# Query projection of a two-block model: keys' split, compressed branch's transposes and scores in other places of the order

## The chip, the cores and the metric

One core of a Trainium2 chip runs the whole program. The metric is the time on the device in microseconds, the median of the runs of one kernel.

## What is computed

Two transformer blocks over 512 tokens of width 1024. The change lies in the attention of the first block's second layer, which has 16 query heads in 4 groups and three branches: a compressed one over 31 blocks of keys, a selected one and a window. With 512 tokens, 8 selected blocks of 64 are all blocks, and the window of 512 takes in all that is past. Cut to what matters:

```python
u = h @ w_q
q = (u[..., :N_HEADS * D_QK] * (D_QK ** -0.5)).reshape(B, S, G, HPG, D_QK)
gates = jax.nn.sigmoid(u[..., N_HEADS * D_QK:] + gate_bias).reshape(B, S, G, HPG, N_BRANCH)
q_rope = apply_partial_rope(q)
...
s_c = jnp.einsum('tghd,cgd->tghc', qn_t, kc_b).astype(jnp.float32)
p_c = masked_softmax(s_c, mask_c)
o_c = jnp.einsum('tghc,cgv->tghv', p_c.astype(vc_b.dtype), vc_b)
...
return g_t[..., 0:1] * o_c + g_t[..., 1:2] * o_s + g_t[..., 2:3] * o_w
```

## The kernel before

The program is one long list of instructions for each engine, written out by hand, with semaphores between them. A product in single precision is made of three: both operands are split into a high part (rounded, on ScalarE) and a low part (the rest, on VectorE), and TensorE adds high x high, low x high and high x low (`three`, lines 619 to 621). The weights come in panels of 1 MB through SyncE's queue into two buffers `a_raw`; `high_a` rounds a panel (line 1451), `low_a` makes its low part (line 2034), and TensorE waits for that (`a_ready`).

**The query projection** has eight panels (pairs of heads, p = 0 to 7, `A_Q + p`). For each, TensorE makes two halves of 24 products, j = 0 and 1, each into a bank of PSUM. VectorE's `evict_q(p)` takes each half out in two instructions, `qb` (line 2439) and `tmp` for the rotation (line 2442). ScalarE copies `qb` (line 1727). GpSimd's `rotate_q(p)` turns the first 24 dimensions of both halves in four instructions (lines 3040 and 3044); ScalarE's `high_q(p)` rounds the pair (`q_hi`, line 1702), VectorE's `low_q(p)` makes the low part (`qb_lo`, line 2448), and GpSimd's `store_q(p)` writes both to memory, from where `stage_q` fetches a pair for the attention. `high_q(p)` and `low_q(p)` stand one pair later in their queues, before the eviction of pair p + 1. The keys `kx` of the two other branches have been made earlier and are split into `kx_hi` (ScalarE, line 1733) and `kx_lo` (VectorE, line 2484), in two pieces.

**The compressed branch** runs between the halves, a group (two pairs) at a time, over one bank, `bank[7]`. For group g: `scores_c(g)` on TensorE (line 963), `copy_scores_c` on ScalarE (`ct`, line 1706), `turn_c` on TensorE, four transposes (line 970), `peak_c` on VectorE (four instructions, lines 2457 to 2461, into `pc`), `expo_c` on ScalarE (line 1710), `weigh_c` on VectorE (five instructions, lines 2465 to 2470), `back_c` on TensorE, four transposes (line 976), `turned_c` on ScalarE (`ptc`, line 1714). Group g's scores come behind the first half of pair 2g + 2 and group 3's in the attention.

**The attention** has 48 units n (a head in three parts); TensorE does `scores(n + 2)`, `turn(n)` (line 1029) and every second unit `outputs` (line 1054), VectorE `peak` (lines 2499 to 2504) and `scale` (line 2515), ScalarE `expo` (line 1741) and `turned` (line 1752). At its start TensorE does

```python
scores(0)
scores_c(GROUPS - 1)
scores(1)
keep(6, 6)
```

where `keep(b, n)` is n filler products into bank b (line 615).

## Time and profile before

| | us |
|---|---|
| median of 3 runs | 2221.01 |
| the runs | 2217.12, 2221.01, 2221.11 |
| the profiled execution | 2217.61 |
| its span in the profile | 2215.8 |

The profile is of one execution, and all its times count from the start of its span. The span lacks 1.8 us of what the device reports for the same execution. PE stands for TensorE, PEld for its weight loads, DVE for VectorE, ACT for ScalarE, POOL for GpSimd. A row of a timeline has the start, the duration, the engine and line, what was written and read, and in brackets how long the engine had been idle and what ended that.

### The profile page before, as it was taken

What the parts mean: (1) busy time and instruction counts of PE and PEld (TensorE: products, weight loads), DVE (VectorE), ACT (ScalarE), POOL (GpSimd) and SP (SyncE); (2) the same over time, 40 slices, a digit from 0 to 9 for tenths busy, and PEclk for the clock granted to TensorE, in tenths of its full rate; (3) what the DMA queues carried; (4) which work ended last, traced back from release to release, by engine and by line L of the source; (5) the groups of instructions that cost most, each with busy time, mean ns of one, the idle gap of its engine ahead of it and who ended that gap; (6) DMA issues with size and microseconds to landing.
All of it is one profiled execution on the core that took longest, in us unless ns stands there. A gap on an engine that the chain in (4) does not pass through costs nothing.

```text
span 2215.8 us, 27265 instructions
## 1 busy us (share of the span) xinstructions
PE 2148.4 (97%) x10514; PEld 1607.1 (73%) x10514; DVE 1270.7 (57%) x1697; ACT 838.2 (38%) x1258; POOL 274.1 (12%) x227
## 2 busy tenths in 40 slices
PE   7999999999999999999999999999999999899998
PEld 6787788888878877777788888877778885233346
DVE  6776855555587678775655555587674463000028
ACT  4556622222253445664422222364442332121243
POOL 1334300000010154000100000010000012222220
PEclk9999999999999999999999999999999999999999
DMA  5222323222224342112322222121122144999961
GB/s 192 88 102 96 114 77 113 85 94 105 78 70 161 124 148 66 39 35 86 126 97 102 85 105 94 66 76 58 58 96 114 58 167 195 414 410 401 376 239 57
DMA packets 60750, 291.84 MB, mean 132 GB/s; under 512 B 13872, under 2 KB 14256, under 8 KB 32582
## 3 DMA queue, kind: packets, MB, share of 16 engines
q1 hardware_dynamic: 41312, 258.49, 30.6%
q0 software_dynamic: 18096, 29.31, 4.4%
q10 hardware_dynamic: 1248, 2.76, 0.3%
q8 instruction: 63, 1.03, 0.2%
q14 instruction: 31, 0.25, 0.0%
HBM read 322.18 MB, written 20.38 MB: 155 GB/s over the span
## 4 chain that ended last, share of the span: by engine, by line
PE 76%; DVE 11%; DMA 5%; ACT 3%; issue 3%; POOL 1%; SPq 0%; ACTq 0%; POOLq 0%; DVEq 0%
PE psum L619 20%; PE psum L621 20%; PE psum L620 20%; PE psum L1353 4%; PE psum L1377 3%; DMA panel<-w_m 3%; PE psum L1054 2%; DVE a_lo L2034 1%; DMA over_panel<-w_m,over_row 1%; PE psum L1029 1%; PE psum L1320 1%; ACT a_hi L1451 1%; PE psum L767 1%; DVE xc L2175 1%; DMA expert_out<-h 1%
## 5 line engine op out<-in xcount | busy, mean ns | idle before, releaser
L619 PE MATMUL psum<-hn_hi,a_hi 128*128 128x512 f32 (+1 forms) x1592 | 631.5, 397 | 7.8 <-DVE hn_lo L2074 3.2
L621 PE MATMUL psum<-hn_hi,a_lo 128*128 128x512 f32 (+1 forms) x1592 | 622.5, 391 | 0.0
L620 PE MATMUL psum<-hn_lo,a_hi 128*128 128x512 f32 (+1 forms) x1592 | 620.2, 390 | 0.0
L619 PEld LDWEIGHTS psum<-hn_hi,a_hi 128*128 128x128 f32 (+1 forms) x1592 | 297.6, 187 | 79.7 <-issue 9.2
L621 PEld LDWEIGHTS psum<-hn_hi,a_lo 128*128 128x128 f32 (+1 forms) x1592 | 297.4, 187 | 68.9
L620 PEld LDWEIGHTS psum<-hn_lo,a_hi 128*128 128x128 f32 (+1 forms) x1592 | 297.4, 187 | 67.7 <-issue 2.4
L2034 DVE TENSOR_TENSOR a_lo<-a_raw,a_hi 128x2048 fp32r<-128x2048 f32 (+1 forms) x110 | 251.7, 2288 | 79.6 <-ACT a_hi L1451 79.0
L1451 ACT ACTIVATE a_hi<-a_raw 128x2048 fp32r<-128x2048 f32 (+1 forms) x110 | 205.2, 1867 | 82.6 <-PE psum L621 70.2
L2118 DVE TENSOR_TENSOR h<-h,psum 128x512 f32<-128x512 f32 x176 | 120.1, 686 | 79.8 <-PE psum L621 79.7
L3006 POOL TENSOR_TENSOR sq<-sq 128x512 f32<-128x512 f32 x6 | 9.0, 1506 | 1151.4 <-ACT sq L1464 1151.4
L2933 DVE TENSOR_TENSOR xhid<-xsg,psum 128x256 f32<-128x256 f32 x24 | 10.1, 421 | 239.9 <-ACT xsg L1984 239.9
L619 PE MATMUL psum<-hid_hi,b_hi 128*128 128x512 f32 x352 | 139.0, 395 | 2.0 <-DVE h L2118 1.9
L621 PE MATMUL psum<-hid_hi,b_lo 128*128 128x512 f32 x352 | 138.0, 392 | 0.0
L1613 ACT ACTIVATE sg<-sg 128x512 f32<-128x512 f32 x44 | 27.8, 632 | 288.3 <-DVE sg L2287 288.3
L620 PE MATMUL psum<-hid_lo,b_hi 128*128 128x512 f32 x352 | 136.7, 388 | 0.0
L1353 PE MATMUL psum<-panel,xw 128*64 128x512 f32 x512 | 115.1, 603 | 2.4 <-ACT xw L1954 2.4
L2292 DVE TENSOR_TENSOR hid<-sg,psum 128x512 f32<-128x512 f32 x44 | 30.2, 687 | 117.2 <-PE psum L621 117.1
L1615 ACT ACTIVATE hid_hi<-hid 128x512 fp32r<-128x512 f32 x44 | 27.8, 632 | 180.9 <-DVE hid L2292 180.9
L1458 ACT ACTIVATE b_hi<-b_raw 128x1024 fp32r<-128x1024 f32 x64 | 66.9, 1050 | 59.6 <-PE psum L621 57.4
L1353 PEld LDWEIGHTS psum<-panel,xw 128*64 128x64 f32 x512 | 36.2, 138 | 70.1 <-issue 70.1
L2040 DVE TENSOR_TENSOR b_lo<-b_raw,b_hi 128x1024 fp32r<-128x1024 f32 x64 | 80.0, 1257 | 7.3 <-ACT b_hi L1458 7.2
L619 PEld LDWEIGHTS psum<-hid_hi,b_hi 128*128 128x128 f32 x352 | 66.2, 188 | 16.7 <-issue 2.5
(524 smaller groups left out, 3337.1 us busy)
## 6 DMA issues: line engine op xcount, KB each, us to landing
a_raw<-w_a SPq DMA_DIRECT2D x116, 1024.0 KB, 4.9
panel<-w_m SPq DMA_DIRECT2D x96, 1024.0 KB, 14.0
b_raw<-w_b SPq DMA_DIRECT2D x64, 512.0 KB, 3.3
q_scratch<-q_hi POOLq DMA_DIRECT2D x7, 384.0 KB, 3.4
q_scratch<-qb_lo POOLq DMA_DIRECT2D x7, 384.0 KB, 4.6
q_hi<-q_scratch POOLq DMA_DIRECT2D x7, 384.0 KB, 4.0
q_lo<-q_scratch POOLq DMA_DIRECT2D x7, 384.0 KB, 4.7
out_t<-h SPq DMA_DIRECT2D x7, 256.0 KB, 2.0
```

Source lines behind the costliest of these rows:

```text
L619: pe.matmul(out, w_hi, x_hi, start=first, stop=False)
L620: pe.matmul(out, w_hi, x_lo, start=False, stop=False)
L621: return pe.matmul(out, w_lo, x_hi, start=False, stop=last)
L1054: mm = pe.matmul(bank[6 + at % 2][side * DV:(side + 1) * DV, t * P:(t + 1) * P], w, x, start=i == 0, stop=i == len(steps) - 1)
L1353: mm = pe.matmul(bank[v][rows, :], xw[:, v, k, rows], w[half][:, k % 4 * 2 * EFF:(k % 4 + 1) * 2 * EFF], start=k == 0, stop=k == KT - 1)
L1377: mm = pe.matmul(bank[4 + 2 * v + hb][rows, :], xturn[:, v, f * P + half * SLOTS:f * P + (half + 1) * SLOTS], w[half][:, f * D + hb * 512: ...
L1451: act.activation(a_hi[s % 2][:, 0:w], a_raw[s % 2][:, 0:w], ACT.Copy).then_inc(a_rounded, 1)
L1458: act.activation(b_hi[s % 2][:, :], b_raw[s % 2][:, :], ACT.Copy).then_inc(b_rounded, 1)
L2034: V.tensor_tensor(a_lo[s % 2][:, 0:w], a_raw[s % 2][:, 0:w], a_hi[s % 2][:, 0:w], ALU.subtract) \
L2040: V.tensor_tensor(b_lo[s % 2][:, :], b_raw[s % 2][:, :], b_hi[s % 2][:, :], ALU.subtract) \
L2118: V.tensor_tensor(h[:, m, :], h[:, m, :], bank[4 + m % 4][:, :], ALU.add).then_inc(y_free, 1)
L2292: V.tensor_tensor(hid[:, f, :], sg[:, f, :], ps[1][:, :], ALU.mult).then_inc(tile_free, 2)
```

## The change

- The keys' split moves from pairs 3 and 4 to pairs 0 and 1, on ScalarE and VectorE.
- `turn_c(g)` moves from behind the second half of pair 2g + 2 to behind the first half of pair 2g + 3; `peak_c(g)` from pair 2g + 2 to pair 2g + 3, `expo_c`, `weigh_c` and `back_c` to pair 2g + 4 (`back_c` behind its second half), `turned_c` to pair 2g + 5.
- `back_c` writes to bank 6 for groups 0 to 2, bank 7 for group 3. `scores_c(g)` then waits for `peak_c(g - 1)` where it waited for `turned_c(g - 1)`.
- `weigh_c(2)`, `back_c(2)` and `turned_c(2)` stand in the attention, `expo_c(2)` before `expo(0)`; the filler products come after `back_c(2)` and go to bank 5.
- In the attention `expo_c(3)` stands at unit 1 (was 2), `weigh_c(3)` at 2 (was 3), `back_c(3)` and `turned_c(3)` at 3 (were 5).

```diff
--- before.py
+++ after.py
@@ -495,6 +495,15 @@
                 return pt_ready, 10 * at + i + 5
             return late_pt_ready, 2 * at + i - 3
 
+        C_ACT = [("copied", 0), ("exp", 0), ("copied", 1), ("turned", 0), ("exp", 1), ("copied", 2), ("turned", 1),
+                 ("exp", 2), ("copied", 3), ("turned", 2), ("exp", 3), ("turned", 3)]
+
+        BACK_C = [6, 6, 6, 7]
+
+        def c_acts(what, g):
+
+            return C_ACT.index((what, g)) + 1
+
         def half_of(half):
             return slice(half * SLOTS, (half + 1) * SLOTS)
 
@@ -957,7 +966,7 @@
                 if g == 0:
                     pe.wait_ge(cmp_done, 2)
                 else:
-                    pe.wait_ge(c_act, 3 * g)
+                    pe.wait_ge(c_dve, 2 * g - 1)
                 for c in range(HPG):
                     pe.wait_ge(base_ready, 8 + 4 * g + c + 1)
                     mm = pe.matmul(bank[7][c * CBLOCK:(c + 1) * CBLOCK, :], kct[:, g * NCMP:g * NCMP + CBLOCK],
@@ -965,15 +974,17 @@
                 mm.then_inc(csc_ready, 1)
 
             def turn_c(g):
-                pe.wait_ge(c_act, 3 * g + 1)
+                pe.wait_ge(c_act, c_acts("copied", g))
                 for t in range(NT):
                     mm = pe.transpose(bank[7][:, t * P:(t + 1) * P], ct[:, t * P:(t + 1) * P], ident)
                 mm.then_inc(ctr_ready, 1)
 
             def back_c(g):
                 pe.wait_ge(c_dve, 2 * g + 2)
+                if 0 < g < GROUPS - 1:
+                    pe.wait_ge(c_act, c_acts("turned", g - 1))
                 for t in range(NT):
-                    mm = pe.transpose(bank[7][:, t * P:(t + 1) * P], pc[:, t, :, :].rearrange("p h c -> p (h c)"), ident)
+                    mm = pe.transpose(bank[BACK_C[g]][:, t * P:(t + 1) * P], pc[:, t, :, :].rearrange("p h c -> p (h c)"), ident)
                 mm.then_inc(ctr_ready, 1)
 
             for p in range(1, NPAIR):
@@ -981,10 +992,12 @@
                 pe.wait_ge(a_ready, s + 1)
                 for j in range(2):
                     product(tile_bank(s, j, s)[:, :], s, j * P, 2 * P, P, hh, hl).then_inc(tile_ready, 1)
-                    if p % 2 == 0:
-                        (turn_c if j else scores_c)(p // 2 - 1)
-                    elif j and p >= 3:
-                        back_c((p - 3) // 2)
+                    if j == 0 and p % 2 == 0:
+                        scores_c(p // 2 - 1)
+                    if j == 0 and p % 2 and p >= 3:
+                        turn_c((p - 3) // 2)
+                    if j == 1 and p % 2 == 0 and p >= 4:
+                        back_c(p // 2 - 2)
 
             def scores(n):
                 u, hd, slot = unit(n)
@@ -1035,9 +1048,8 @@
                 pair = PAIR_AT[at]
                 g = pair // 2
                 if u == 0:
-                    pe.wait_ge(c_act, 3 * (g + 1))
-                    if at == 1:
-                        pe.wait_ge(c_act, 3 * GROUPS)
+                    if at < 2:
+                        pe.wait_ge(c_act, c_acts("turned", GROUPS - 2 + at))
                     if at >= 2:
                         pe.wait_ge(o_split, at - 1)
                 for side in range(2):
@@ -1066,15 +1078,16 @@
             scores(0)
             scores_c(GROUPS - 1)
             scores(1)
-            keep(6, 6)
+            back_c(GROUPS - 2)
+            keep(5, 6)
             for n in range(NUNIT):
                 if n + 2 < NUNIT:
                     scores(n + 2)
                 if n == 0:
                     turn_c(GROUPS - 1)
-                if n == 5:
+                turn(n)
+                if n == 3:
                     back_c(GROUPS - 1)
-                turn(n)
                 if n % 2 == 0 and n >= 2:
                     outputs(n // 2 - 1)
             pe.wait_ge(a_ready, A_WO + 1)
@@ -1711,26 +1724,26 @@
 
             def turned_c(g):
                 act.wait_ge(ctr_ready, 2 * g + 2)
-                act.activation(ptc[:, g, :], bank[7][:, :], ACT.Copy).then_inc(c_act, 1)
+                act.activation(ptc[:, g, :], bank[BACK_C[g]][:, :], ACT.Copy).then_inc(c_act, 1)
 
             for p in range(NPAIR):
                 if p:
                     high_a(A_Q + p + 1)
-                if p % 2 and p >= 3:
-                    expo_c((p - 3) // 2)
                 if p % 2 == 0 and p >= 4:
-                    turned_c(p // 2 - 2)
+                    expo_c(p // 2 - 2)
                 if p:
                     high_q(p - 1)
+                if p % 2 and p >= 5:
+                    turned_c((p - 5) // 2)
                 for j in range(2):
                     act.wait_ge(base_ready, 8 + 2 * p + j + 1)
                     act.activation(qb[:, 2 * (p % 2) + j, 1, :], qb[:, 2 * (p % 2) + j, 0, :], ACT.Copy) \
                        .then_inc(base_copied, 1)
-                    if j == 0 and p % 2 == 0 and p:
-                        copy_scores_c(p // 2 - 1)
-                if p in (3, 4):
+                if p % 2 == 0 and p:
+                    copy_scores_c(p // 2 - 1)
+                if p < 2:
                     act.wait_ge(rope_done, 8)
-                    act.activation(kx_hi[:, p - 3, :, :], kx[:, p - 3, :, :], ACT.Copy).then_inc(k_rounded, 1)
+                    act.activation(kx_hi[:, p, :, :], kx[:, p, :, :], ACT.Copy).then_inc(k_rounded, 1)
 
             def expo(n):
                 act.wait_ge(mx_done, n + 1)
@@ -1755,19 +1768,20 @@
                 act.wait_ge(o_ready, 3 * at + 3)
                 act.activation(hn_hi[:, PAIR_AT[at], :], bank[6 + at % 2][:, :], ACT.Copy).then_inc(o_rounded, 1)
 
-            turned_c(GROUPS - 2)
+            expo_c(GROUPS - 2)
             expo(0)
             copy_scores_c(GROUPS - 1)
             expo(1)
+            turned_c(GROUPS - 2)
             for n in range(NUNIT):
                 turned(n)
                 if n + 2 < NUNIT:
                     expo(n + 2)
                 if n == 0:
                     high_q(NPAIR - 1)
-                if n == 2:
+                if n == 1:
                     expo_c(GROUPS - 1)
-                if n == 5:
+                if n == 3:
                     turned_c(GROUPS - 1)
                 if n % 6 == 1 and n > 6:
                     high_out(n // 6 - 1)
@@ -2472,17 +2486,13 @@
             for p in range(NPAIR):
                 if p:
                     low_a(A_Q + p + 1)
-                if p % 2 and p >= 3:
-                    weigh_c((p - 3) // 2)
+                if p % 2 == 0 and p >= 4:
+                    weigh_c(p // 2 - 2)
                 if p:
                     low_q(p - 1)
                 evict_q(p)
-                if p % 2 == 0 and p >= 2:
-                    peak_c(p // 2 - 1)
-                if p in (3, 4):
-                    V.wait_ge(k_rounded, p - 2)
-                    V.tensor_tensor(kx_lo[:, p - 3, :, :], kx[:, p - 3, :, :], kx_hi[:, p - 3, :, :], ALU.subtract) \
-                     .then_inc(k_split, 1)
+                if p % 2 and p >= 3:
+                    peak_c((p - 3) // 2)
                 if p == 0:
                     V.wait_ge(cmp_w2, 2)
                     V.wait_ge(rows_zero, 1)
@@ -2491,6 +2501,9 @@
                                             .rearrange("p (g c) -> p g c", g=GROUPS))
                     ins.then_inc(cmp_done, 1)
                     V.wait_ge(small_out, 3)
+                if p < 2:
+                    V.wait_ge(k_rounded, p + 1)
+                    V.tensor_tensor(kx_lo[:, p, :, :], kx[:, p, :, :], kx_hi[:, p, :, :], ALU.subtract).then_inc(k_split, 1)
 
             def peak(n):
                 v, u, x = n % 2, unit(n)[0], ast[:, n % 4, :]
@@ -2528,6 +2541,7 @@
                  .then_inc(o_split, 1)
 
             peak(0)
+            weigh_c(GROUPS - 2)
             peak(1)
             scale(0)
             for n in range(NUNIT):
@@ -2541,7 +2555,7 @@
                     peak_c(GROUPS - 1)
                 if n == 1:
                     low_q(NPAIR - 1)
-                if n == 3:
+                if n == 2:
                     weigh_c(GROUPS - 1)
                 if n % 6 == 1 and n > 6:
                     low_out(n // 6 - 1)
```

Three places of the order, first VectorE in pairs 0 and 1 (`kx_lo` is the keys' low part, `a_lo` the low part of a panel, `qb_lo` that of a pair of queries). Before:

```order
L2490 COPY vcz<-psum 31x4x64 x3
L2034 TENSOR_TENSOR a_lo<-a_raw,a_hi 128x2048 [waits a_rounded,small_out]
L2448 TENSOR_TENSOR qb_lo<-qb,q_hi 96x2x512 [waits queries_rounded]
L2439 SCALAR_TENSOR_TENSOR qb<-psum,rn 96x512 [waits tile_ready]
L2442 SCALAR_TENSOR_TENSOR tmp<-psum,cs 24x512 [waits rope_done]
L2439 SCALAR_TENSOR_TENSOR qb<-psum,rn 96x512 [waits tile_ready]
L2442 SCALAR_TENSOR_TENSOR tmp<-psum,cs 24x512 [waits rope_done]
```

And with the change:

```order
L2500 COPY vcz<-psum 31x4x64 x3
L2506 TENSOR_TENSOR kx_lo<-kx,kx_hi 96x2048 [waits keys_rounded,small_out]
L2048 TENSOR_TENSOR a_lo<-a_raw,a_hi 128x2048 [waits a_rounded]
L2462 TENSOR_TENSOR qb_lo<-qb,q_hi 96x2x512 [waits queries_rounded]
L2453 SCALAR_TENSOR_TENSOR qb<-psum,rn 96x512 [waits tile_ready]
L2456 SCALAR_TENSOR_TENSOR tmp<-psum,cs 24x512 [waits rope_done]
L2453 SCALAR_TENSOR_TENSOR qb<-psum,rn 96x512 [waits tile_ready]
L2456 SCALAR_TENSOR_TENSOR tmp<-psum,cs 24x512 [waits rope_done]
L2506 TENSOR_TENSOR kx_lo<-kx,kx_hi 96x2048 [waits keys_rounded]
L2048 TENSOR_TENSOR a_lo<-a_raw,a_hi 128x2048 [waits a_rounded]
```

The two `kx_lo` now stand directly before the `a_lo` of panels 2 and 3; the rest of the piece is as it was.

VectorE from pair 7 into the attention (`pc` and `cst` belong to the compressed branch, `ast` to the attention's units). Before:

```order
L2465 TENSOR_REDUCE cst<-pc 128x16 [waits c_act]
L2466 TENSOR_SCALAR cst<-cst 128x16 [waits dve_step]
L2467 RECIPROCAL cst<-cst 128x16 [waits dve_step]
L2469 TENSOR_TENSOR cst<-cst,gates 128x16 [waits dve_step]
L2470 TENSOR_TENSOR pc<-pc,cst 128x512 [waits dve_step]
L2448 TENSOR_TENSOR qb_lo<-qb,q_hi 96x2x512 [waits queries_rounded]
L2439 SCALAR_TENSOR_TENSOR qb<-psum,rn 96x512 [waits tile_ready,csc_ready,q_stored1]
L2442 SCALAR_TENSOR_TENSOR tmp<-psum,cs 24x512 [waits rope_done]
L2439 SCALAR_TENSOR_TENSOR qb<-psum,rn 96x512 [waits tile_ready]
L2442 SCALAR_TENSOR_TENSOR tmp<-psum,cs 24x512 [waits rope_done]
L2499 TENSOR_REDUCE ast<-psum 128x2 [waits sc_ready]
```

And with the change:

```order
L2456 SCALAR_TENSOR_TENSOR tmp<-psum,cs 24x512 [waits rope_done]
L2471 TENSOR_TENSOR pc<-psum,cn 128x512 [waits ctr_ready]
L2473 TENSOR_REDUCE cst<-pc 128x16 [waits dve_step]
L2474 TENSOR_SCALAR cst<-cst 128x16 [waits dve_step]
L2475 TENSOR_TENSOR pc<-pc,cst 128x512 [waits dve_step]
L2512 TENSOR_REDUCE ast<-psum 128x2 [waits sc_ready]
L2514 TENSOR_REDUCE ast<-psum 128x2
L2479 TENSOR_REDUCE cst<-pc 128x16 [waits c_act]
L2480 TENSOR_SCALAR cst<-cst 128x16 [waits dve_step]
L2481 RECIPROCAL cst<-cst 128x16 [waits dve_step]
L2483 TENSOR_TENSOR cst<-cst,gates 128x16 [waits dve_step]
L2484 TENSOR_TENSOR pc<-pc,cst 128x512 [waits dve_step]
```

`peak_c(2)` (the first four rows behind `tmp`) now stands between the last eviction and the attention's first unit, and `weigh_c(2)` (the last five) behind that unit's `peak`.

TensorE at the start of the attention, with the change (`qb,kct` are the compressed scores of group 3, `kx` and `q` the attention's, `cn,pc` the transposes of `back_c(2)`):

```order
L972 MATMUL psum<-qb,kct 32x512 [waits base_ready,c_dve]
L972 MATMUL psum<-qb,kct 32x512 [waits base_ready] x3
L628 MATMUL psum<-kx_hi,q_hi 128x256 [waits tile_free]
L629 MATMUL psum<-kx_lo,q_hi 128x256
L630 MATMUL psum<-kx_hi,q_lo 128x256
L628 MATMUL psum<-kx_hi,q_hi 128x512
L629 MATMUL psum<-kx_lo,q_hi 128x512
L630 MATMUL psum<-kx_hi,q_lo 128x512
L1031 MATMUL psum<-masks 128x256
L1031 MATMUL psum<-masks 128x2x128
L987 MATMUL psum<-cn,pc 128x128 [waits c_act,c_dve]
L987 MATMUL psum<-cn,pc 128x128 x3
```

Before, the first of these rows waited for `c_act` (`turned_c(2)`) and not for `c_dve` (`peak_c(2)`), and the `cn,pc` rows stood ahead of the attention's first scores.

## Rows read from the trace of the kernel before

**Rows 1.** Page, head and part 1: busy us, share of the span, instructions
```profile
span 2215.8 us, 27265 instructions
...
PE 2148.4 (97%) x10514; PEld 1607.1 (73%) x10514; DVE 1270.7 (57%) x1697; ACT 838.2 (38%) x1258; POOL 274.1 (12%) x227
```

**Rows 2.** Waits of TensorE, 755 to 900 us: total, times, longest (us)
```profile
PE psum L970 <- ACT ct L1706: 3.0, 2, 2.5
```

**Rows 3.** Timeline of TensorE, 784 to 864 us: start, us, line, operation, idle before
```profile
785.49 0.50 PE L619 MATMUL psum<-hn_hi,a_hi 128*128 128x512 f32 x1
...
791.11 0.60 PE L970 MATMUL psum<-cn,ct 128*128 128x128 f32 x4
...
791.46 0.48 PE L619 MATMUL psum<-hn_hi,a_hi 128*128 128x512 f32 x1
...
817.88 0.66 PE L970 MATMUL psum<-cn,ct 128*128 128x128 f32 x4 [2.52 <-ACT ct L1706]
...
858.49 1.07 PE L963 MATMUL psum<-qb,kct 96*32 96x512 f32 x8 [0.83 <-ACT ptc L1714]
...
860.88 2.76 PE L615 MATMUL psum<-cn 128*128 128x256 f32 x12
...
863.28 0.53 PE L619 MATMUL psum<-kx_hi,q_hi 96*128 96x384 f32 x1
```

**Rows 4.** Windows: length, busy us of the five rows of engines, PEclk, DMA share, GB/s
```profile
49.20:54.40 5.20, 5.18 (x18) 3.80 (x19) 1.10 (x1) 2.51 (x4) 2.94 (x2) 0.50 0.55 195
...
819.00:822.40 3.40, 3.40 (x10) 2.58 (x10) 3.30 (x5) 3.39 (x2) 3.16 (x3) 0.53 0.45 118
...
872.00:876.00 4.00, 4.00 (x46) 3.25 (x45) 2.63 (x6) 2.75 (x7) 0.00 (x0) 1.00 0.02 4
...
876.07:896.92 20.85, 19.76 (x190) 16.20 (x189) 16.70 (x39) 14.11 (x44) 1.31 (x2) 1.00 0.18 39
```

**Rows 5.** Timeline of GpSimd, 766 to 815 us
```profile
770.43 3.17 POOL L3044 TENSOR_TENSOR qb<-tmp,sq 24x512 f32<-24x512 f32 x1 [0.17 <-POOL sq L3040]
...
802.60 0.63 POOL L3053 DMA_DIRECT2D q_hi<-q_scratch  x1
...
806.62 5.55 POOL L3040 TENSOR_TENSOR sq<-qb,cs 24x512 f32<-24x512 f32 x1
```

**Rows 6.** Instructions on tile tmp, 760 to 870 us: min/median/max in ns
```profile
L3044 POOL TENSOR_TENSOR qb<-tmp,sq x16: 1253/1286/3171, 767.7 to 861.0; 24x512 f32<-24x512 f32 x16
```

**Rows 7.** Timeline of VectorE, 766 to 860 us
```profile
774.73 1.22 DVE L2448 TENSOR_TENSOR qb_lo<-qb,q_hi 96x1024 fp32r<-96x1024 f32 x1 [2.28 <-ACT q_hi L1702]
...
805.94 2.86 DVE L2484 TENSOR_TENSOR kx_lo<-kx,kx_hi 96x2048 fp32r<-96x2048 f32 x1 [1.78 <-ACT kx_hi L1733]
...
808.72 2.28 DVE L2034 TENSOR_TENSOR a_lo<-a_raw,a_hi 128x2048 fp32r<-128x2048 f32 x1
...
829.82 1.22 DVE L2448 TENSOR_TENSOR qb_lo<-qb,q_hi 96x1024 fp32r<-96x1024 f32 x1
...
841.13 1.22 DVE L2448 TENSOR_TENSOR qb_lo<-qb,q_hi 96x1024 fp32r<-96x1024 f32 x1 [2.27 <-ACT q_hi L1702]
...
848.08 0.69 DVE L2461 TENSOR_TENSOR pc<-pc,cst 128x512 f32<-128x512 f32 x1
...
851.99 0.68 DVE L2465 TENSOR_REDUCE cst<-pc 128x16 f32<-128x512 f32 x1
...
854.03 1.21 DVE L2448 TENSOR_TENSOR qb_lo<-qb,q_hi 96x1024 fp32r<-96x1024 f32 x1
...
858.04 0.42 DVE L2499 TENSOR_REDUCE ast<-psum 128x2 f32<-128x256 f32 x1
```

**Rows 8.** Timeline of ScalarE, 766 to 860 us
```profile
813.65 1.06 ACT L1702 ACTIVATE q_hi<-qb 96x1024 fp32r<-96x1024 f32 x1 [5.47 <-POOL qb L3044]
```

**Rows 9.** Timeline of TensorE, its stops elsewhere: idle time in brackets
```profile
49.22 0.76 PE L774 MATMUL psum<-xc_hi,a_hi 64*128 64x512 f32 x1 [3.75 <-issue]
...
871.34 0.87 PE L1029 MATMUL psum<-cn,pm_b 128*128 128x128 f32 x6 [1.69 <-DVE pm_b L2515]
```

## The prediction

> **What bounds the kernel now.** I read four views, in this order. The page's first part says whose time the span is: TensorE is busy 97% of 2215.8 us [rows 1], so only what TensorE waits for can be won. The waits of TensorE from 755 us to 900 us, the stretch of the query projection and the start of the attention, say what there is, above all 3.0 us in two waits of the transposes (L970) for `ct` [rows 2]. The timeline of TensorE shows where and when: the long one, 2.52 us, stands before the transposes of group 1 at 817.88, and the 0.83 us before the last compressed scores at 858.49 [rows 3]. The windows with the granted clock show a second loss behind the long wait: 0.53 in 819.0 to 822.4, that is half of 2.4 GHz [rows 4]. Three hi/lo products there are 0.6 us longer each, about 1.6 us in all. So at most 2.52 + 0.48 + 1.6 + 0.83 = 5.4 us can go, of 2217.61.
>
> Then I ask what was late. `ct` of group 1 stands in ScalarE's queue behind a copy that needs pair 4's eviction, that behind `low_q(3)` on VectorE, that behind `q_hi` at 813.65, which had waited 5.47 us for GpSimd [rows 8]. GpSimd's rotation of pair 3 had one instruction of 5.55 us at 806.62 [rows 5], where its like have a median of 1.29 [rows 6]: it ends 1.2 us behind VectorE's `kx_lo` and `a_lo`, which ran back to back from 805.94 to 811.0 [rows 7]. So there is a ring: `low_q(p-1)`, eviction of pair p, store and rotation on GpSimd, `q_hi` on ScalarE, `low_q(p)`. Its length is the distance of two `qb_lo` rows, 11.3 us (829.82 to 841.13) with one ordinary `a_lo` in GpSimd's way, and 12.9 us (841.13 to 854.03) where `peak_c`, `a_lo` and `weigh_c` lie in VectorE's queue between them [rows 7]. A pair on TensorE takes two halves of 5.6 us (785.49 to 791.11) plus 0.35 us per group of transposes and 1.0 per compressed scores (1.07 in the row at 858.49) [rows 3], 11.4 to 12.6 us. The ring is as long as TensorE's pair, and it is this ring that I follow through the change.
>
> **The change, part by part.** No instruction is added or removed on TensorE, VectorE or GpSimd, nor on ScalarE; what changes is where they stand and what they wait for.
>
> *Keys' split in pairs 0 and 1.* `kx_hi` (1.9 us) delays `a_hi` by as much, and TensorE needs those panels 3 us later still, so that costs nothing; if that cover went, it would be 1.9 us a panel. On VectorE `kx_lo` (2.3 us alone) now lies directly before `a_lo`. GpSimd's blocked instruction at 770.43 took 3.17 us behind one `a_lo` [rows 5]; with `kx_lo` ahead of it it ends 2.2 us later. `low_q(0)`, at 774.73 [rows 7], goes to 776.9. In pair 1 the instruction is blocked by both, as at 806.62: 4.24 us instead of 1.87, and the interval to `low_q(1)` is 11.3 + 2.4 = 13.7 us.
>
> Here the Trainium skill speaks otherwise. In "SBUF — State Buffer", section "Who interferes with whom", a VectorE instruction with two SBUF inputs and a GpSimd instruction that reads SBUF exclude each other, whoever is first holding the ports "for the whole instruction". By that GpSimd would be let in after `kx_lo`; the row at 806.62 shows it held over both. The sum goes by the row, the page's rule is rival 2.
>
> *The ring after that.* To `low_q(2)` 11.3; to `low_q(3)` with `peak_c(0)`, `a_lo`, `weigh_c(0)` between them, as in the 12.9 row, and `stage_q(0)` on GpSimd: between 12.9 and 12.9 + 1.3 (two DMA issues of 0.63) [rows 5], and I take 13.0, since VectorE sets that interval and not GpSimd; then 11.3, 12.9, 11.3. Sum from 776.9: 13.7 + 11.3 + 13.0 + 11.3 + 12.9 + 11.3 = 73.5, so `low_q(6)` begins at 850.4, 3.6 us earlier than the 854.03 of before. The kernel loses its two late `kx_lo` and wins 3.6 us on VectorE.
>
> *TensorE in the projection.* It starts pair 3 at 791.1 without the transposes before it and would need 11.44 us for each odd pair and 12.6 for each even one: 3 x 11.44 + 2 x 12.6 = 59.5, to 850.6. The transposes wait for copies half a panel old: `ct` of group 1 is written at about 819.5, they come at 822, so the 2.52, the 0.48 and the 1.6 us of the clock go. But `scores_c(g)` now waits for `peak_c(g-1)`, which ends 7.64 us behind the start of the `low_q` before it (841.13 to 848.77) [rows 7]. For group 1 that is 801.9 + 7.6 = 809.5 where TensorE arrives at 808.0: 1.5 us of new wait. For group 2 826.2 + 7.6 = 833.8 against 833.6: 0.2. The other bank for `back_c` is free for them all and costs nothing.
>
> *The passage into the attention, which decides.* `peak_c(2)` now stands on VectorE behind the eviction of the last pair: 850.4 + 7.6 = 858.0. TensorE has done the projection at 852.3 and `scores(0)` at 853.6, and then stands before `scores_c(3)` until 858.0: 4.4 us. Behind it in the queue are `scores(1)`, `back_c(2)` and the six filler products. VectorE goes on with `peak(0)` (1.05 us, its first row at 858.04) and `weigh_c(2)` (2.1, from 851.99 to 854.03) [rows 7], to 861.2; `back_c(2)` waits for it, 0.4; the fillers take 2.4 (860.88 to 863.28) [rows 3]; `scores(2)` begins at 864.0. Before it was 863.28. **+0.7 us**: the bank's wait of before (858.49) and the new one (858.0) are at the same place, and `weigh_c(2)`, formerly under the projection, now stands before the fillers.
>
> *The clock.* The nearest row to a stop of 4.4 us is that of 3.75 us before 49.22 [rows 9]: the clock is at 0.50 for 5.2 us under work behind it [rows 4]; behind 2.52 us it was 3.4 us, and behind the 1.69 us before 871.34 [rows 9] it stayed at 1.00 [rows 4]. Bounds: 0 and 3.4 us (6.8 us at half). I take the 3.75 row: in 5.2 us TensorE does 2.6 us of work, so at 863.2 it is where it would be at 861.4 without the fall (0.8 us of it is wait anyway). **+1.8 us.**
>
> *The last group in the attention.* `weigh_c(3)` one unit earlier, `back_c(3)` two. TensorE is idle for 1.09 us of the 20.85 us from 876.07 [rows 4], so 1 us is the bound on either side; VectorE's 2.1 us before `peak(5)` may add 0.7 at `turn(4)`, and what left later units gives it back: 0.
>
> Sum: 0.7 + 1.8 = +2.5, 2217.61 + 2.5 = 2220.1 us in the terms of the profiled execution. Its time lies 3.4 us under the median of the runs shown, 2221.01, so the prediction for a median is 2223.5 us. Two of the four times lie at 2217 and two at 2221, a scatter larger than the effect; 0.2%, 4.4 us, is what a measurement of this kernel can tell from no change.
>
> **The rivals.**
> 1. *No fall of the clock.* The stop begins at another moment than that before 49.22 did. For it: 1.7 us in the attention brought none. Against: both stops over 2.5 us did. 2221.01 + 0.7 = 2221.7.
> 2. *GpSimd is let in between `kx_lo` and `a_lo`.* Both early delays shrink by 2.3, but `a_lo` then stands behind GpSimd's 1.3: 1.0 us each, `peak_c(2)` ends at 856.0, `scores(2)` at 862.0, -1.3, with the clock's 1.8: 2221.5. This is the rule of the SBUF page above; row 806.62 is against it.
> 3. *TensorE regains the lead.* If the ring is shorter than my intervals, the floor is the last half of the projection: 850.9, then eviction 1.4 and `peak_c` 2.9, 855.2; `scores(2)` at 861.2, -2.1, with a stop short enough for no fall: 2218.9. The order of VectorE's queue excludes more; to pass -4.4 something that I put at nothing has to give as well.
> 4. *Slower.* One mechanism: GpSimd's rotations of pairs 6 and 7 meet VectorE in `peak_c(2)` and `weigh_c(2)`, which now lie in their time. It decides if `stage_q` costs its full 1.2 and one rotation (1.3) holds a step of VectorE; the stop becomes 6.9 us, the clock's fall then lies wholly under work and costs 3.4 - 0.8 = 2.6. 0.7 + 1.2 + 1.3 + 2.6 = 5.8: 2226.8. For it: the two engines do exclude each other in the rows; against: `peak_c` of 3.5 us has such a hold in it already.
>
> **How the numbers follow.** Forecast 0.47, rival 1 0.17, rival 2 0.12, rival 3 0.12, rival 4 0.12. Likeliest: 2223.5. The range leaves out the slow end of rival 4 and the fast end of rival 3: 2217.5 to 2227.5. Slower by over 0.2% (above 2225.4) is rival 4 and a little of the forecast, 0.16; faster by over 0.2% (below 2216.6) is a part of rival 3, 0.07; the rest, 0.77, is within.
>
> **What would show it.** Right: no wait of `cn,ct` transposes on TensorE and no half clock at 819; a wait of about 1.5 us before `scores_c(1)`, one of about 4.4 us before `scores_c(3)` ended by VectorE's `pc`, one of 0.7 before `back_c(2)`, then half clock; two GpSimd instructions of 3 to 5 us in pairs 0 and 1; `scores(2)` within 3 us of 863.3. Wrong: `peak_c(2)` done before 855, or `scores(2)` before 861; a loss outside 755 to 900 us would be none of mine.

## The result and the profile after

The change has a median of 2225.38 us (2222.41 to 2231.92, 14 runs) beside 2222.23 us for the kernel before (2217.12 to 2226.42, 14 runs): a ratio of 1.0022, 95% interval 1.0013 to 1.0031, or 3 to 7 us slower. Two repetitions gave 1.0023 [1.0013, 1.0033] and 1.0006 [0.9994, 1.0018]. All 38 executions of the change together have a mean of 2225.80, all 123 of the kernel before 2221.97: a difference of 3.8 us, 0.17%. The profiled execution of the change took 2224.76 us. "Half clock" below is a stretch in which the profile grants TensorE 0.50 of 2.4 GHz, 1.2 GHz.

The page's first part, which answers to [rows 1]: TensorE is busy 5 us longer, in a span 7.2 us longer, with as many instructions.

```profile
span 2223.0 us, 27260 instructions
...
PE 2153.5 (97%) x10514; PEld 1611.8 (73%) x10514; DVE 1272.2 (57%) x1697; ACT 838.8 (38%) x1258; POOL 281.8 (13%) x227
```

The waits of TensorE from 755 to 900 us, as in [rows 2] (total, times, longest). The waits for `ct` (3.0 us) and for `ptc` (0.83) are gone; waits for `pc`, written by `peak_c`, have come, 5.5 us against 3.8.

```profile
PE psum L972 <- DVE pc L2475: 5.5, 3, 4.2
PE psum L1042 <- DVE pm_b L2528: 2.2, 2, 1.7
```

**How two executions are laid beside each other.** The whole program reaches the projection up to 4 us earlier or later from one execution to another, so absolute times mislead. I count from the first eviction of pair 0, which precedes all that the change moves. The kernel before:

```profile
765.46 0.69 DVE L2439 SCALAR_TENSOR_TENSOR qb<-psum,rn 96x512 f32<-96x512 f32 x1 [0.26 <-DVE gates L2426]
...
1022.28 1.09 PE L1029 MATMUL psum<-cn,pm_b 128*128 128x128 f32 x8 [1.77 <-DVE pm_b L2515]
```

and the same two rows after, the second being a row of the attention's last unit:

```profile
764.69 0.69 DVE L2453 SCALAR_TENSOR_TENSOR qb<-psum,rn 96x512 f32<-96x512 f32 x1 [0.26 <-DVE gates L2440]
...
1025.03 1.09 PE L1042 MATMUL psum<-cn,pm_b 128*128 128x128 f32 x8 [1.77 <-DVE pm_b L2528]
```

From the first to the second the kernel before takes 256.82 us and the change 260.34: **3.5 us are lost between them**, about the loss in the medians (3.2) and in the means (3.8). The kernel before has one profile, so how far its own distance varies from one execution to another isn't shown. The rest of the profiled execution's 7.2 us is a half clock at 1026.3, which is not in every execution, and the last 400 us, where half clocks lie elsewhere in each execution.

TensorE's timeline, answering to [rows 3] and to the second row of [rows 9]:

```profile
808.56 1.07 PE L972 MATMUL psum<-qb,kct 96*32 96x512 f32 x8 [1.12 <-DVE pc L2475]
...
832.96 1.07 PE L972 MATMUL psum<-qb,kct 96*32 96x512 f32 x8 [0.24 <-DVE pc L2475]
...
857.05 1.94 PE L972 MATMUL psum<-qb,kct 96*32 96x512 f32 x8 [4.15 <-DVE pc L2475]
...
861.46 1.06 PE L987 MATMUL psum<-cn,pc 128*128 128x128 f32 x4
862.31 2.83 PE L624 MATMUL psum<-cn 128*128 128x256 f32 x12
864.79 0.53 PE L628 MATMUL psum<-kx_hi,q_hi 96*128 96x384 f32 x1
...
872.83 1.54 PE L1042 MATMUL psum<-cn,pm_b 128*128 128x128 f32 x6 [1.73 <-DVE pm_b L2528]
```

and its clock (length, busy time of the five rows of engines, granted clock, DMA), answering to [rows 4]:

```profile
819.00:822.40 3.40, 3.40 (x18) 2.81 (x18) 2.02 (x1) 1.34 (x1) 3.23 (x3) 1.00 0.29 75
855.60:862.40 6.80, 5.35 (x21) 3.01 (x22) 4.89 (x11) 2.84 (x10) 2.36 (x2) 0.50 0.01 2
872.70:876.10 3.40, 3.27 (x24) 2.94 (x26) 3.36 (x7) 2.90 (x8) 0.00 (x0) 0.50 0.03 5
1026.30:1029.70 3.40, 3.40 (x31) 3.07 (x28) 0.88 (x2) 0.08 (x1) 0.00 (x0) 0.50 0.00 0
```

The clock at 819 is full now. In its place there is 1.2 GHz from 855.6 to 862.4, begun during the stop of 4.15 us, and once more from 872.7 to 876.1, behind a stop of 1.73 us. The kernel before had a stop of 1.69 us at that place [rows 9], with the clock at 1.00 behind it [rows 4].

Split by rows: `scores(2)` begins 100.10 us behind the first eviction (97.82 before, from [rows 3]), +2.28. The transposes at 872.83 are at 108.14 (105.88 before), +2.26. The last unit is at +3.52. So 2.3 us are lost in the passage and 1.3 us behind 872.83, where the second half clock is.

All executions together agree. Each has its mean granted clock on record: 0.9915 over the 38 of the change, 0.9931 over the 109 of the kernel before for which it is given, 0.9931 over the 11 with the stop filled (below). By an estimate from these means (twice what the clock lacks, times the span) an execution of the change has 38 us at half clock and one of the kernel before 30; the profiles show 10.2 us against 3.4 between the two rows. Half of the 7.5 us of difference, 3.7 us, is what it costs if all of it lies under work: as much as the whole loss.

### The profile page after: what moved, and what is told of

It reads as the page before. It is cut to its first block, busy times and chain, and to the rows that moved or that the text cites. A ratio compares the mean times of both kernels' runs of the same rounds, so it can differ in the third digit from the quotient of the medians.

```text
span 2223.0 us, 27260 instructions
## 1 busy us (share of the span) xinstructions
PE 2153.5 (97%) x10514; PEld 1611.8 (73%) x10514; DVE 1272.2 (57%) x1697; ACT 838.8 (38%) x1258; POOL 281.8 (13%) x227
## 4 chain that ended last, share of the span: by engine, by line
PE 75%; DVE 11%; DMA 5%; ACT 3%; POOL 3%; issue 3%; SPq 0%; POOLq 0%; ACTq 0%; DVEq 0%
PE psum L628 19%; PE psum L630 19%; PE psum L629 19%; PE psum L1366 4%; DMA panel<-w_m 3%; PE psum L1390 3%; PE psum L1066 2%; DVE a_lo L2048 2%; POOL qb L3058 1%; PE psum L1042 1%; PE psum L1333 1%; ACT a_hi L1464 1%; PE psum L776 1%; DVE xc L2189 1%; DMA expert_out<-h 1%
```

## The experiments

Twelve runs. In each profile I read three things: the distance from the first eviction to `scores(2)`, that to the last unit's row, and where between them the clock was at half.

| kernel | scores(2) | last unit | half clock between, us | ratio to before |
|---|---|---|---|---|
| before | 97.8 | 256.8 | 3.4 at 819 | |
| the change | 100.1 | 260.3 | 6.8 at 856, 3.4 at 873 | 1.0022 [1.0013, 1.0031] |
| again | 100.5 | 260.7 | the same two | 1.0023 [1.0013, 1.0033] |
| a third time | 100.2 | 260.5 | the same two | 1.0006 [0.9994, 1.0018] |
| stop filled | 98.3 | 257.4 | none | 1.0003 [0.9992, 1.0015] |
| no fillers | 97.5 | 257.0 | 6.8 at 859 | 1.0003 [0.9994, 1.0012] |
| keys back in pairs 3, 4 | 100.7 | 260.9 | 3.4 at 841, 865, 878 | 1.0023 [1.0011, 1.0035] |
| keys' move alone | 97.1 | 257.7 | 3.4 at 872 | 0.9999 [0.9989, 1.0009] |
| change, keys earlier still | 96.4 | 255.5 | 3.4 at 855 | 1.0002 [0.9986, 1.0018] |
| group 2 as before | 94.6 | 255.0 | 3.4 at 869 | 0.9984 [0.9973, 0.9996] |
| once more | 94.6 | 253.7 | none | 0.9993 [0.9983, 1.0004] |
| that, keys earlier still | 91.9 | 250.9 | none | 0.9970 [0.9957, 0.9982] |
| once more | 91.9 | 251.0 | none | 0.9977 [0.9960, 0.9994] |
| that, no fillers | 90.4 | 250.3 | none | 0.9966 [0.9947, 0.9984] |

Each version's distance to the last unit, less the 256.8 of before, agrees with its ratio (0.0010 is 2.2 us) to 2.5 us. That is the scatter of the ratios: one of eight to fourteen runs of the same version moves by up to 0.17% from one set to the next, the distance by 0.4 us, or 1.3 us where a half clock comes or not. In the versions with the keys earlier still, `kx_lo` lies ahead of the first eviction, but it doesn't delay it: the row of VectorE ahead of both (`sd`, at 754.67 in the kernel before) lies 10.8 us before the eviction with the edit and without.

**The change again.**

> The changed kernel once more, on the same chip as the three that follow. Theory P (passage): the loss is one stop of TensorE of about 4.2 us before the compressed scores of group 3, ended by peak_c(2), with 0.9 us of a wait for weigh_c(2) and a fall of the clock behind it; scores(2) begins 2 to 2.5 us later than before, counted from the first eviction of pair 0. Theory K (keys): the loss is made by the keys' split in pairs 0 and 1. Theory C (clock elsewhere): half of it or more comes from falls of the clock at other stops, which move from execution to execution. All three expect 1.0013 to 1.0031 of before. C expects the falls behind 862 us to lie at other places than in the first profile; P and K that the passage is the same within 0.3 us.

The stop before `scores_c(3)` was 4.17 us, the half clocks at 856.5 and 873.6, and none at 1026. The passage is the same to 0.4 us in the three executions of the change; `scores(2)` is 2.7 us later than in the kernel before, a little over what theory P put, and its 0.9 us of wait for `weigh_c(2)` isn't there. Theory C fails for the 3.5 us: both falls of the clock stand where they stood.

**The stop filled.** Nine filler products more, in front of `scores_c(3)`:

```diff
             scores(0)
+            keep(5, 9)
             scores_c(GROUPS - 1)
```

> The change with nine filler products (0.4 us each, 3.6 us) into bank 5 between scores(0) and the compressed scores of group 3, where TensorE stands for 4.2 us. The end of the stop is set by peak_c(2) on VectorE in any case. Theory P: the clock stays at 1.00 at the passage, the compressed scores begin at the same time, and scores(2) comes 1.2 to 1.8 us earlier than in the change, so 1.0005 to 1.0015 of before. Theory K: fillers change nothing, 1.0022. If the fillers last longer than the stop, it would be slower by what is over, under 0.5 us.

```profile
856.44 4.05 PE L624 MATMUL psum<-cn 128*128 128x256 f32 x18
860.80 1.07 PE L972 MATMUL psum<-qb,kct 96*32 96x512 f32 x8 [0.32 <-DVE pc L2476]
...
863.77 0.66 PE L987 MATMUL psum<-cn,pc 128*128 128x128 f32 x4 [0.41 <-DVE pc L2485]
864.26 2.75 PE L624 MATMUL psum<-cn 128*128 128x256 f32 x12
```

Nothing useful is done earlier (`scores_c(3)` begins 92.41 us behind the first eviction, 92.36 in the change), and yet `scores(2)` comes 1.8 us earlier than in the change and the last unit 2.96 us: both half clocks are gone. The transposes of `back_c(2)` now stand in the 0.41 us wait for `weigh_c(2)` that I had predicted. Without the half clocks the change costs 0.5 us at `scores(2)`, and the ratio is 1.0003, under the 1.0005 to 1.0015 that I had expected. The loss is thus mostly the clock behind the stop, and not the stop.

**No fillers.** The change without its six filler products:

```diff
             back_c(GROUPS - 2)
-            keep(5, 6)
             for n in range(NUNIT):
```

> The change without the six filler products behind back_c(2). Theory P (the passage costs what stands in TensorE's queue behind the stop of 4.2 us): scores(2) 2.4 to 2.8 us earlier than in the change (about 862), but turn(0) then waits for ScalarE's exp and VectorE's scale by about as much, so the time is within 1 us of the change, ratio to before 1.0015 to 1.0030. Rival (the fillers are pure loss behind so long a stop): ratio 1.0005 to 1.0015, 2 us less than the change. A second rival, on the clock: with another wait of 2 us the clock falls longer, ratio above 1.0030.

```profile
859.25 1.93 PE L972 MATMUL psum<-qb,kct 96*32 96x512 f32 x8 [4.13 <-DVE pc L2474]
...
863.65 1.06 PE L987 MATMUL psum<-cn,pc 128*128 128x128 f32 x4
864.36 0.67 PE L628 MATMUL psum<-kx_hi,q_hi 96*128 96x384 f32 x1
...
872.84 0.88 PE L1042 MATMUL psum<-cn,pm_b 128*128 128x128 f32 x6 [1.73 <-DVE pm_b L2527]
```

My theory P fell, and its rival came nearer: it said 1.0005 to 1.0015, and the ratio is 1.0003. `scores(2)` is 2.6 us earlier, and only 0.4 us of that is taken back: the row of `pm_b`, 1.73 us of wait in both kernels, is 2.2 us earlier, and behind it the clock stayed at 1.00. Why it stayed there isn't shown; with the 1.1 us that this gives, the last unit is 3.3 us earlier. The stop is as long (4.13) and the half clock too (6.8 us). Behind so late an arrival, six filler products are work in the way: their 2.4 us were a term of my sum that I took as given.

**The keys back in pairs 3 and 4**, the change otherwise kept:

```diff
-                if p < 2:
+                if p in (3, 4):
                     act.wait_ge(rope_done, 8)
...
-                if p < 2:
-                    V.wait_ge(k_rounded, p + 1)
+                if p in (3, 4):
+                    V.wait_ge(k_rounded, p - 2)
```

> The change with the keys' split back in pairs 3 and 4, all else as changed. Theory P, by the ring: the late kx_lo lengthen the intervals of low_q(2) to low_q(3) to about 15.4 us and of the next to 13.7, so that peak_c(2) ends about 2.5 us later than in the change and so does scores(2): 1.003 to 1.0045 of before. Theory K: the loss goes with the early split, 1.000 of before, peak_c(2) earlier than in the change.

```profile
839.09 1.07 PE L972 MATMUL psum<-qb,kct 96*32 96x512 f32 x8 [2.79 <-DVE pc L2475]
...
863.36 1.06 PE L972 MATMUL psum<-qb,kct 96*32 96x512 f32 x8 [2.74 <-DVE pc L2475]
```

The same 5.5 us of wait, cut into two stops of 2.8 us, each with 3.4 us at half clock. Theory K fell: without the early keys the loss is the same, 1.0023. Theory P missed too: `peak_c(2)` ends 1.5 us later than in the change and not 2.5, `scores(2)` 0.2 to 0.6 us later, and 1.003 was the least that it had put. The place of the keys' split moves the wait and does not remove it. `low_q(6)` begins 84.8 us behind the first eviction in the change, 86.2 here, and 82.0 with `kx_lo` out of the ring (below): by the three, `kx_lo` costs the chain 2.8 us in pairs 0 and 1 and 4.2 us in pairs 3 and 4.

**The keys' move alone**, on the kernel before (the same two edits, the other way, and nothing of the compressed branch moved).

> The kernel before with one edit: the keys' split of pairs 3 and 4 moved to pairs 0 and 1, as in the change; the compressed branch stays as it was. Theory K (the stop of 2.52 us at 817.88 comes from kx_lo in VectorE's queue of pair 3 alone, and the moved transposes are not needed for it): low_q(4) near 826 instead of 829.8, the stop before the transposes of group 1 under 0.6 us, no half clock at 819, scores(2) near 860 to 861 (863.28 before), ratio to before 0.9980 to 0.9990. Rival, theory T (the transposes half a panel earlier are late for ct anyway, because each copy stands behind an eviction): a stop of 1 to 2.5 us remains there, scores(2) within 1 us of 863.3 and ratio 0.9995 to 1.0005.

```profile
794.58 0.66 PE L970 MATMUL psum<-cn,ct 128*128 128x128 f32 x4 [2.40 <-ACT ct L1706]
...
820.21 0.66 PE L970 MATMUL psum<-cn,ct 128*128 128x128 f32 x4 [1.34 <-ACT ct L1706]
```

The two waits for `ct` are 2.40 us, before group 0's transposes, and 1.34, before group 1's; in the kernel before they were 2.52, before group 1's, and 0.48, before group 2's. The clock stayed at 1.00 behind both. Theory T held: `scores(2)` is 0.75 us earlier than before and the time is the kernel's before, 0.9999. So of the two halves of the change the keys' move alone brings nothing, and the moves of the compressed branch alone (the run above) lose as much as the whole.

**Group 2 as before.** The change, with group 2's transposes behind pair 6's second half, `peak_c(2)` in pair 6, `weigh_c(2)` and `back_c(2)` in pair 7, the latter to bank 6 (TensorE's part; ScalarE's and VectorE's follow it):

```diff
-                    if j == 0 and p % 2 and p >= 3:
+                    if j == 0 and p in (3, 5):
                         turn_c((p - 3) // 2)
-                    if j == 1 and p % 2 == 0 and p >= 4:
+                    if j == 1 and p in (4, 6):
                         back_c(p // 2 - 2)
+                    if j == 1 and p == 6:
+                        turn_c(2)
+                    if j == 1 and p == 7:
+                        back_c(2)
...
-            back_c(GROUPS - 2)
             keep(5, 6)
```

> The change with group 2's chain as before: scores, transposes and peak_c(2) in pair 6, exp and weigh_c(2) in pair 7, its last transposes behind the second half of pair 7 (into bank 6); keys, groups 0, 1 and 3 as in the change. Theory P: the 4.2 us stop goes, TensorE waits only for the last eviction (under 2 us), no fall of the clock at the passage, scores(2) begins about 859 to 860, 3 to 4 us before the kernel before; 0.998 to 0.999 of before. Theory K: the ring that the keys have lengthened still sets the end of the projection; scores(2) not earlier than before, 1.000 to 1.002.

```profile
841.71 0.66 PE L979 MATMUL psum<-cn,ct 128*128 128x128 f32 x4 [0.98 <-ACT ct L1722]
...
855.01 1.06 PE L972 MATMUL psum<-qb,kct 96*32 96x512 f32 x8
857.41 2.76 PE L624 MATMUL psum<-cn 128*128 128x256 f32 x12
859.81 0.53 PE L628 MATMUL psum<-kx_hi,q_hi 96*128 96x384 f32 x1
```

No wait before `scores_c(3)`, where the change had 4.15 us; a wait of 0.98 for `ct` is the price, and those of 1.16 and 0.29 before `scores_c(1)` and `scores_c(2)` stay. `scores(2)` is 3.2 us earlier than in the kernel before and 5.5 earlier than in the change. Once more, beside other kernels:

> The kernel of the run in which group 2's chain stays where it was before (its transposes behind pair 6, back_c(2) behind pair 7), once more, on another chip or hour: if its gain is real, ratio 0.9975 to 0.9995 again, scores(2) near 860 (863.28 before). If the gain was scatter of the clock's falls, 0.9995 or above.

The ratio, 0.9993, is in the range expected, but its interval includes 1. The projection is the same to 0.1 us, and the two executions show what a half clock behind the 1.7 us stop costs: one had it, the other not (length, busy, clock, as above; first the earlier run, then the later):

```profile
868.70:872.10 3.40, 3.40 (x33) 3.16 (x32) 3.29 (x8) 2.13 (x6) 0.00 (x0) 0.52 0.02 5
```

```profile
867.50:870.90 3.40, 3.40 (x41) 2.89 (x40) 3.33 (x7) 2.50 (x7) 0.00 (x0) 1.00 0.02 5
```

Their last units are at 255.0 and 253.7: **1.3 us**, the same as the change loses behind 872.83.

**The keys' split earlier still**, first on the change: `kx_hi` between the roundings of the projection's first two panels, `kx_lo` on VectorE before the low part of the second, where both engines stood idle for over 7 us.

```diff
             high_a(A_Q)
+            act.wait_ge(rope_done, 8)
+            for i in range(2):
+                act.activation(kx_hi[:, i, :, :], kx[:, i, :, :], ACT.Copy).then_inc(k_rounded, 1)
             high_a(A_Q + 1)
...
+            for i in range(2):
+                V.wait_ge(k_rounded, i + 1)
+                V.tensor_tensor(kx_lo[:, i, :, :], kx[:, i, :, :], kx_hi[:, i, :, :], ALU.subtract).then_inc(k_split, 1)
             low_a(A_Q + 1)
```

> The change, with the keys' split one place earlier still: kx_hi between the roundings of the first two panels, kx_lo ahead of them on VectorE, out of the way of low_q(0) and low_q(1). Theory P (the stop of 4.2 us before scores_c(3) is the ring of low_q, begun 2.2 us late and with one interval 2.4 us long): low_q(6) some 3 to 4.5 us earlier in the run's own terms, peak_c(2) ends by as much earlier, the stop before scores_c(3) 0 to 1.5 us, no half clock behind it, scores(2) 96.3 to 97.5 us behind the first qb of pair 0 (100.1 to 100.5 in the change, 97.8 before), ratio to before 0.9985 to 1.0000. Rival (the end of the projection on TensorE is late by its own work and the eviction of pair 7 with peak_c(2) behind it is what counts): the stop stays at 3 us or more, ratio above 1.0010.

VectorE's `qb_lo` rows, one per pair:

```profile
774.10 1.22 DVE L2465 TENSOR_TENSOR qb_lo<-qb,q_hi 96x1024 fp32r<-96x1024 f32 x1 [2.28 <-ACT q_hi L1718]
...
784.59 1.21 DVE L2465 TENSOR_TENSOR qb_lo<-qb,q_hi 96x1024 fp32r<-96x1024 f32 x1
...
796.55 1.21 DVE L2465 TENSOR_TENSOR qb_lo<-qb,q_hi 96x1024 fp32r<-96x1024 f32 x1
...
802.11 0.69 DVE L2456 SCALAR_TENSOR_TENSOR qb<-psum,rn 96x512 f32<-96x512 f32 x1 [2.91 <-PE psum L630]
...
811.06 1.22 DVE L2465 TENSOR_TENSOR qb_lo<-qb,q_hi 96x1024 fp32r<-96x1024 f32 x1
```

`low_q(0)` and `low_q(1)` are earlier as expected, and the interval that was 13.6 is 10.5. GpSimd is held over one instruction only:

```profile
769.80 3.17 POOL L3058 TENSOR_TENSOR qb<-tmp,sq 24x512 f32<-24x512 f32 x1 [0.17 <-POOL sq L3054]
```

Then VectorE is so early that it waits for TensorE (the row at 802.11), and with `peak_c(0)` and `weigh_c(0)` behind that, `low_q(3)` comes 14.5 us after `low_q(2)`: the ring is no longer what binds. `low_q(6)` is 2.8 us earlier, and not 3 to 4.5. The stop before `scores_c(3)` is 2.88, not under 1.5, and the half clock behind it 3.4 us. Still `scores(2)` is 3.7 us earlier than in the change, and the last unit 1.3 us earlier than in the kernel before. The ratio, 1.0002 with an interval from 0.9986 to 1.0018, is too wide to show that.

Then the same edit on the version with group 2 as before:

> As last_back, and the keys' split one place earlier still: kx_hi between the roundings of the first two panels of the projection, kx_lo behind the eviction ahead of it, where ScalarE was idle 8.3 us and VectorE 7.3 us. Theory R (low_q(0) and the ring of low_q, eviction, GpSimd, q_hi set TensorE's end of the projection): low_q(0) 2 us earlier and the first interval 11.3 instead of 13.6, so low_q(2) 4 us earlier, no wait before scores_c(1), scores(2) 1 to 2 us earlier than in last_back, ratio to before 0.9970 to 0.9980. Rival (TensorE's own work is the bound once the two stops are gone): scores(2) within 0.5 us of last_back's, same ratio.

TensorE's waits from 755 to 900 us, behind the projection's start:

```profile
PE psum L1046 <- DVE pm_b L2532: 2.7, 3, 1.7
PE psum L628 <- DVE a_lo L2052: 1.6, 1, 1.6
```

The 1.6 us for `a_lo` stand at 754.9, ahead of the first eviction, and 1.4 to 1.5 us do so in the kernel before and in the change. No wait for `ct`, `pc` or `ptc` is left, the clock is at 1.00 from 850 to 876, and `scores(2)` is 2.8 us earlier than without the edit; theory R held there, though by another road than its 11.3 us. Twice beside the kernel before, 0.9970 and 0.9977: **5 to 7 us faster than the kernel before**, and by the means of all executions (2216.53, 20 runs, against 2225.80, 38 runs) 9 us faster than the change.

> The version that beat both, once more. If its gain is real: ratio 0.9962 to 0.9980, scores(2) 91.9 us behind the first qb of pair 0 (97.8 before). If it was scatter: above 0.9985.

And without the fillers:

> The same version without its six filler products. Theory F (the fillers are a loss of 2.2 us only where the clock is at half from a stop before them; at full clock they fill a wait that turn(0) has anyway): scores(2) 2.4 us earlier, but the first transposes of pm_a wait by 1 to 2.4 us more, time within 1 us of the version with fillers, or 1 to 2 us slower where the clock falls behind that wait. Rival (the fillers are a loss everywhere): ratio lower by 0.0008 to 0.0012 than with them.

`scores(2)` is 1.5 us earlier, the last unit 0.7; waits of 0.75, 0.60 and 0.18 us have come in their place, a part of the 2.4 us. Here TensorE comes to unit 0 before its `pm_a` is ready, and the fillers mostly cover that wait, as theory F said; in the change it came late and they covered none. The 0.7 us are within the 1 us that theory F put. But the version without fillers has the lower ratio by 0.0004 and, against the run beside it, 0.0011, which is what the rival put (0.0008 to 0.0012); both lie within the intervals. Which is faster is open.

**The change a third time.**

> The change itself, a third execution. Open is the half clock behind the wait of 1.7 us for pm_b, 14 us into the attention: it stood in both profiles of the change and in the one with the keys put back, in neither with the fillers before scores_c(3) nor without fillers, and in one of two of last_back. Theory A (it belongs to the stop and the half clock of the passage, so the change has it each time): half clock for 3.4 us near 873, the row of pm_b at the end of the attention 260 to 261 us behind the first qb of pair 0 (256.8 before), ratio 1.0015 to 1.0030. Rival B (such a fall comes by chance, in some executions of any order): none near 873 this time, that row near 259.3, and the ratio of many runs between 1.0010 and 1.0022.

The half clock stood at 873.8 again, and the last unit at 260.5. Three of three executions of the change have it, and the one with the keys put back; that speaks for theory A. But the ratio, 1.0006, is below what both theories expected, and the keys' move alone and one of two executions with group 2 as before have the same half clock without any stop of 4 us. So the passage makes it likelier at most; what decides it is open.

## Why the prediction came out as it did

The forecast case came true: 2.5 us slower was put, and it is 3.2 us by the medians and 3.8 us by all executions. Its size was up to 1.3 us short.

- *What goes.* The 2.52, the 0.48 and the half clock at 819 went, as said.
- *The ring.* `low_q(0)` predicted at 776.9, found at 776.16 in an execution that runs 0.77 us ahead: 776.93. The intervals were put at 13.7, 11.3, 13.0, 11.3, 12.9, 11.3, and VectorE's rows give 13.6, 11.3, 13.1, 11.3, 12.7, 11.3:

```profile
776.16 1.22 DVE L2462 TENSOR_TENSOR qb_lo<-qb,q_hi 96x1024 fp32r<-96x1024 f32 x1 [2.27 <-ACT q_hi L1715]
...
789.75 1.22 DVE L2462 TENSOR_TENSOR qb_lo<-qb,q_hi 96x1024 fp32r<-96x1024 f32 x1 [2.27 <-ACT q_hi L1715]
801.07 1.22 DVE L2462 TENSOR_TENSOR qb_lo<-qb,q_hi 96x1024 fp32r<-96x1024 f32 x1 [2.27 <-ACT q_hi L1715]
...
814.13 1.22 DVE L2462 TENSOR_TENSOR qb_lo<-qb,q_hi 96x1024 fp32r<-96x1024 f32 x1
825.45 1.22 DVE L2462 TENSOR_TENSOR qb_lo<-qb,q_hi 96x1024 fp32r<-96x1024 f32 x1 [2.27 <-ACT q_hi L1715]
...
838.14 1.21 DVE L2462 TENSOR_TENSOR qb_lo<-qb,q_hi 96x1024 fp32r<-96x1024 f32 x1
849.45 1.22 DVE L2462 TENSOR_TENSOR qb_lo<-qb,q_hi 96x1024 fp32r<-96x1024 f32 x1 [2.27 <-ACT q_hi L1715]
```

- *Rival 2, GpSimd let in between.* Not so. GpSimd's rotations of pairs 0 and 1 were held over `kx_lo` and `a_lo` both:

```profile
769.67 5.37 POOL L3058 TENSOR_TENSOR qb<-tmp,sq 24x512 f32<-24x512 f32 x1 [0.17 <-POOL sq L3054]
...
783.29 5.33 POOL L3058 TENSOR_TENSOR qb<-tmp,sq 24x512 f32<-24x512 f32 x1 [0.17 <-POOL sq L3054]
```

 Without `kx_lo` there, in the version with the keys earlier still, the first of them took 3.17 us, the 2.2 us less that I had put. By the Trainium skill ("SBUF — State Buffer", "Who interferes with whom") whoever issues first gets the shared ports for the whole instruction and the other blocks. The rows agree with the blocking, but show GpSimd held over two VectorE instructions in a row.
- *The waits.* 1.5, 0.2 and 4.4 us were predicted before the three compressed scores; 1.12, 0.24 and 4.15 were found.
- *The passage.* +0.7 and the clock's +1.8 were predicted together as +2.5 at `scores(2)`; +2.28 was found. How they divide is shown by the filled stop: +0.5 without the clock, and 1.8 for it. The prediction gave the wait before `back_c(2)` three sizes: 0.4 in the sum, 0.8 in the clock's term, 0.7 among the signs; with the stop filled it is 0.41. In the change it isn't there, since `scores_c(3)` and `scores(1)` at half clock took until 861.46, past the end of `weigh_c(2)` at 859.96. The half clock lasted 6.8 us and not the 5.2 of the nearest row; 5.35 us of it had work in it. That the term still came out at 1.8 is partly luck: the stretch was put too short and the wait inside it too long.
- *Rivals 3 and 4.* Not so. The ring was not shorter: `low_q(6)` begins at 849.45, 850.2 when the 0.77 us are added, 850.4 predicted. Nor did GpSimd hold VectorE further: `peak_c(2)` ends at 857.0, 857.8 so counted, against 858.0, and `weigh_c(2)` takes 2.1 us as before.
- *Rival 1, no fall of the clock.* Not so; but its price was right: the filled stop gave 1.0003, where 2221.7 had been set beside 2221.01.
- *The step that was short: "behind the 1.69 us before 871.34 it stayed at 1.00", and with it "the last group in the attention: 0".* The last group's move did cost nothing: from the row of `pm_b` to the last unit the change without fillers takes 151.09 us and the one with the stop filled 151.05, the kernel before 150.94. But the change takes 152.20, with the clock at half in 3.4 us of it. I had one execution, in which a stop of this size brought no half clock, and gave it no chance in any other. It is 1.3 us, a term put at nothing, and it makes +2.5 into +3.5 to +3.9 in three executions, beside the 3.8 between the means.
- *The base.* I set 2221.01 under the sum. The 123 executions of the kernel before have a mean of 2221.97; the other 3.4 us to 2225.4 are the change's loss.
- *Same or slower.* I gave "within 0.2%" 0.77 and "slower" 0.16. The measured loss, 0.17% by all executions and 0.22% by the first fourteen, lies on the line between them.

## What to carry to other kernels

A stop of TensorE has two prices, its length and the clock behind it. Filling a stop of 4 us with products whose results nobody uses won 3 us here without any work coming earlier, and the same kind of products behind a stop, where the next work was already waiting, cost 2 us: whether fillers pay is a question of where they stand. To move work out of a chain's way helps only where that chain is then not late again: the change cleared pairs 4 to 6 and put the last group at the one place where nothing was left to cover it, and moved the keys' split to another place of the same ring. Group 2 left where it was, with the keys' split in a gap that lay outside the ring, gave 5 to 7 us, where I had counted at most 5.4 in the profile.

## What was not expected of the hardware

- A stop of 1.7 us sometimes has 3.4 us of half clock behind it and sometimes none, in the same program and at the same place: with group 2 as before one execution of two, 1.3 us apart. At 1026.3, behind a stop of 1.77 us, the profiled execution of the change and its third one have it, the second has not; the kernel with the keys' move alone has it too (at 1025.2), so it doesn't need the change's stop of 4 us. In the profiled one the first product behind the attention is at 1030.19 us, 5.1 us later behind the first eviction than in the kernel before (1025.83), where the last unit was 3.5 later: that half clock cost 1.6 us.
- The stop of 2.40 us before group 0's transposes in the kernel with the keys' move alone brought no half clock, that of 2.52 in the kernel before did [rows 3, 4]. The length of the stop alone does not tell.
- GpSimd was held over two VectorE instructions in a row three times in the two kernels (5.55 [rows 5], 5.37 and 5.33 us) and a fourth time with the keys back in pairs 3 and 4 (5.33 us).
